# A fused two-layer transformer step: the join of three attention groups by token and in two fp32r parts, and the scan's input sent to DRAM one slot sooner

## The chip, the core and the metric

The kernel runs on one core of one Trainium2 chip. A core has TensorE (matmuls), VectorE, ScalarE and GpSimd, and SyncE, whose queue here issues all DMAs. The metric is the time of one execution on the device in microseconds (us): 1775.94 us for the kernel before, the median of three runs from 1772.67 to 1776.62.

## What is computed

Two layers on one sequence of 1024 tokens of width 1024. The first one has a branch with three groups of four heads of dilated causal attention. Each group gives, for each token and head, a normalised output and the logarithm of its denominator; the groups are then joined by a softmax over these logarithms:

```python
for gi, (window, dilation) in enumerate(B_PATTERNS):      # three groups
    hs = slice(gi * B_HEADS_PER_GROUP, (gi + 1) * B_HEADS_PER_GROUP)
    o_g, lse_g = dilated_window_attention(q[:, :, hs], k[:, :, hs], v[:, :, hs],
                                          rel_bias[:, hs], dilation, window // dilation)
    outs.append(o_g)
    lses.append(lse_g)
o_all = jnp.stack(outs, axis=0)
wts = jax.nn.softmax(jnp.stack(lses, axis=0), axis=0)
y_b = jnp.sum(wts[..., None] * o_all, axis=0).reshape(bn, s, B_OUT_WIDTH).astype(x.dtype)
y_b = y_b * jax.nn.silu(b_z)
```

The second layer has a complex diagonal state space model (the "scan") over an input `u` of 16 groups of 16 channels, next to two kinds of attention. All projections of both layers (`h @ w_in` and the like) are matmuls in float32, and they are most of the work.

## The kernel before

A program is a few *runs* of the class `Dense`, each a row of *slots*. A slot is one half (512 tokens) of one 128-column weight tile: 24 matmuls of 128x128 by 128x512 on L93. Data and weights are each split into a high part rounded to fp32r, the one-instruction float32 format of TensorE ("dense"), and an fp32r remainder; a product is the sum of three partial products over 8 pieces of depth, hence 24. A weight tile comes by DMA (L196) into one buffer `w_raw`; ScalarE rounds its high part (L210) and VectorE takes the remainder (L221). The tile of slots 2n and 2n+1 is prepared this way while earlier ones are multiplied.

All other work hangs on the slots: objects of class `Beside` have a method for each engine that is called at each slot `s`. Each engine's program is the concatenation of these calls in a fixed written order, so the order on an engine never changes at run time; engines meet only at semaphores. On SyncE, `sync(s)` comes before the load of the weight tile that is due at the end of slot `s`. On VectorE a slot has first the `vector_early` calls, then the remainder of the next-but-one weight tile (L221, in the second slot of a tile), then the `vector` calls. On ScalarE a slot has first `scalar_early`, then waits for the slot's matmuls, moves their result (L330) and frees the PSUM bank, rounds a weight tile (L210), and then calls `scalar`. On TensorE the 24 matmuls come first and the `tensor` calls behind them.

The object `Join` sits in the run `Middle`, in its slots 1 and 3 to 8 (`FIRST` = 1, and its own count starts there):

- Slot 1, VectorE (`masks`): the maxima and sums of groups 1 and 2, kept per token in residue order, are spread by masks into operands (L1266, L1272). TensorE: a transpose (L1218) and 12 matmuls (L1222) for the maxima and as many for the sums bring them into 32 rows (8 token tiles x 4 heads) by 128 tokens, for each of the three groups. `places` holds the permutations; `join_sel` is a table of ones that picks a head's row.
- Slot 1, VectorE (`weights`, L1287 to L1297) and ScalarE (one Exp, L1302): the softmax over the groups in the 32x384 layout.
- Slots 3 to 8, one for each of three groups by two pairs of heads, TensorE (L1232): 8 plain float32 matmuls of depth 32 copy a weight to the 64 channels of its head, for 128 tokens each, into banks 2 and 3. VectorE multiplies the group's output by it (L1248), adds up (L1253) and, in the last group, multiplies by the gate (L1256). ScalarE's activation of the first tile that overwrites the groups' outputs waits for the last of it (semaphore `done`).

In the same slots `Modulation` streams 32 parts of `ada_w` (two a slot, L1718), which VectorE multiplies and adds (L1751, L1755).

The object `Ssm` sits in the last run. The first two weight tiles make `u` (slots 0 to 3). SyncE writes `u` to DRAM (L2415) and reads it back in another layout in 8 DMAs (L2420); the matmuls behind slot 7 (L2463) are the first that need it. In that run `self.first` is 7, so the write stands at slot 4 (`i == -3`) and the read at slot 5 (`i == -2`).

Of the kernel before, what the change touches and what calls it, by code (L numbers as in the profile page):

```python
# [16 lines left out]
P = 128  # L17
# [1157 lines left out]
class Join(Beside):  # L1175
# [5 lines left out]
    PLACES = 12 * P + 12  # L1181
    FIRST = 1

    def __init__(self, core, places_dram, sel_dram, maxima, sums, oT, ybT, ident, room):
        self.core, self.places_dram, self.sel_dram, self.ident = core, places_dram, sel_dram, ident
        self.maxima, self.sums, self.oT, self.ybT = maxima, sums, oT, ybT
# [3 lines left out]
        def take(n):  # L1190
            at[0] += n
            return flat[:, at[0] - n:at[0]]

        self.places = take(self.PLACES)
        self.put = self.places[:, 0:12 * P].rearrange("p (n q) -> p n q", q=P)
        self.mask = self.places[:, 12 * P:12 * P + 12]
        self.sel = take(16 * P)[0:32].rearrange("p (t a f) -> p t a f", t=TT, a=2)
        self.spaced = [[take(r * 32).rearrange("p (n t h) -> p n t h", n=r, t=TT) for r in (4, 8)] for _ in range(2)]
        self.m = take(3 * P)[0:32].rearrange("p (g q) -> p g q", g=3)
        self.e = take(3 * P)[0:32].rearrange("p (g q) -> p g q", g=3)  # L1200
        self.top = take(P)[0:32]
        self.loaded, self.masked, self.placed, self.chain, self.topped, self.exped, self.ready, self.spread, \
            self.used, self.done = (core.sem("join_" + n) for n in (
                "loaded", "masked", "placed", "chain", "topped", "exped", "ready", "spread", "used", "done"))

    def turned(self, w):
        return bank(self.core, 6 + w, 1)[0:32, 0:3 * P].rearrange("p (g q) -> p g q", g=3)

    def sync(self, sp, s):
        if s == -1:  # L1210
            sp.dma_start(self.places, self.places_dram).then_inc(self.loaded, 16)
            sp.dma_start(self.sel.rearrange("p t a f -> p (t a f)"), self.sel_dram).then_inc(self.loaded, 16)
# [2476 lines left out]
```

## Time and profile before

| | |
|---|---|
| median of three runs | 1775.94 us (1772.67 to 1776.62) |
| profiled execution: its own time | 1770.18 us |
| its span, first to last instruction | 1768.5 us |
| TensorE busy with matmuls | 1732.2 us, 98% |
| VectorE / ScalarE / GpSimd busy | 52% / 37% / 14% |
| mean granted TensorE clock | 0.997 of 2.4 GHz |
| moved by DMA | 123.10 MB, 70 GB/s on average |

The profile is of one execution. In a timeline each row is a stretch of like instructions: when it starts, how long it lasts, the engine, the line of the kernel, the operation, the tiles as out<-in with their shapes, the count, and, in brackets, how long the engine stood idle before it and what ended that. PE is TensorE's matmul part and PEld its weight loads, which run beside the matmuls. A plain float32 matmul is recorded as two instructions, one with fp32r operands as one. The duration of one matmul is its passage through the array; the distance from one start to the next is what it costs in a stream.

### The profile page before, as it was taken

To read this page: it belongs to the slowest core of one execution; us is meant where nothing else is said; L and a number is where in the kernel's file an instruction comes from. 1 tells how busy PE (TensorE), PEld (TensorE's weight loads), DVE (VectorE), ACT (ScalarE), POOL (GpSimd) and SP (SyncE) were. 2 spreads that over 40 slices of the span, in tenths; PEclk is the share of its full clock that TensorE was granted. 3 is DMA by queue.
4 is the path that set the end of the run, shared out by engine and by line. 5 is a ranking of instruction groups with operands and counts; after the bars stand their busy time and mean duration, and the time that the engine had idled before them with its cause. 6 is when DMAs were issued, how large, how long until landed. Compare 5 with 4: busy or idle time off the path is not lost.

```text
span 1768.5 us, 22516 instructions
## 1 busy us (share of the span) xinstructions
PE 1732.2 (98%) x8828; PEld 1405.8 (79%) x8828; DVE 914.2 (52%) x1525; ACT 652.8 (37%) x1223; POOL 245.4 (14%) x412
## 2 busy tenths in 40 slices
PE   7999999999999999999999999999999999999998
PEld 6788877788888888778888788888787777777786
DVE  5158868564435744763222322467152455657764
ACT  5234438512334432752112211233313463444731
POOL 3012210288701100000000000481000000000000
PEclk9999999999999999999999999999999999999999
DMA  4221110346332200311111221232713111001133
GB/s 144 60 66 48 38 35 2 121 126 190 101 123 62 71 25 13 93 30 48 54 38 55 66 63 30 95 134 85 151 36 99 37 37 37 22 27 48 37 131 107
DMA packets 148277, 123.10 MB, mean 70 GB/s; under 512 B 10556, under 2 KB 133803, under 8 KB 147499
## 3 DMA queue, kind: packets, MB, share of 16 engines
q1 hardware_dynamic: 148170, 121.65, 22.9%
q8 instruction: 71, 1.16, 0.3%
q14 instruction: 36, 0.29, 0.1%
HBM read 108.37 MB, written 13.26 MB: 69 GB/s over the span
## 4 chain that ended last, share of the span: by engine, by line
PE 50%; DVE 4%; DMA 3%; ACT 1%; issue 1%; SPq 0%; DVEq 0%; ACTq 0%
PE psum L93 28%; PE psum L278 7%; PE psum L81 7%; PE psum L2667 2%; PE psum L2698 2%; PE psum L2681 1%; PE psum L1680 1%; DMA w_raw<-w_in 1%; DMA w_raw<-w_out 1%; DMA ssm_U<-u_scratch 0%; PE psum L945 0%; PE psum L931 0%; DVE h2T L2300 0%; PE psum L2463 0%; DVE w_parts L221 0%
## 5 line engine op out<-in xcount | busy, mean ns | idle before, releaser
L93 PE MATMUL psum<-hT,w_parts 128*128 128x512 f32 x3360 | 794.9, 393 | 6.5 <-PEq L61 3.4
L93 PEld LDWEIGHTS psum<-hT,w_parts 128*128 128x128 f32 x3360 | 628.5, 188 | 142.2 <-issue 6.1
L221 DVE TENSOR_TENSOR w_parts<-w_raw,w_parts 128x1024 fp32r<-128x1024 f32 x88 | 111.5, 1267 | 371.9 <-ACT w_parts L210 371.9
L93 PE MATMUL psum<-h2T,w_parts 128*128 128x512 f32 x1248 | 297.1, 394 | 0.0
L93 PEld LDWEIGHTS psum<-h2T,w_parts 128*128 128x128 f32 x1248 | 230.8, 188 | 48.4 <-issue 1.7
L1474 ACT ACTIVATE gate<-psum,cols 128x512 f32<-128x512 f32 x48 | 33.0, 688 | 284.5 <-PE psum L81 284.5
L81 PE MATMUL psum<-y_high,wp_parts 128*128 128x512 f32 x384 | 128.8, 395 | 0.5 <-DVE ya_low L1532 0.3
L210 ACT CAST w_parts<-w_raw 128x1024 fp32r<-128x1024 f32 x88 | 91.6, 1041 | 33.5 <-DMA w_raw<-w_in 28.9
L81 PEld LDWEIGHTS psum<-y_high,wp_parts 128*128 128x128 f32 x384 | 72.0, 188 | 19.2 <-DVE wp_parts L1522 1.7
L278 PE MATMUL psum<-w_parts,y_parts 128*128 128x512 f32 x360 | 82.6, 390 | 0.6 <-DVE w_parts L271 0.6
L403 DVE RECIPROCAL x<-x 128x512 f32<-128x512 f32 x24 | 80.2, 3343 | 0.0
L278 PEld LDWEIGHTS psum<-w_parts,y_parts 128*128 128x128 f32 x360 | 67.3, 188 | 15.1 <-DVE w_parts L271 1.0
L2862 ACT ACTIVATE diff_p<-diff_p,diff_small 128x128 f32<-128x128 f32 (+7 forms) x64 | 49.2, 770 | 81.5 <-DVE diff_small L2792 81.4
L278 PE MATMUL psum<-w_parts,merged_high 128*128 128x512 f32 x240 | 76.0, 392 | 0.0
L1486 DVE TENSOR_TENSOR gate<-psum,gate 128x512 f32<-128x512 f32 x32 | 22.0, 688 | 80.5 <-ACT gate L1474 80.5
L2788 DVE CUSTOM_DVE_ANT_0 diff_p<-psum,far 128x128 f32<-128x128 f32 (+7 forms) x64 | 45.8, 753 | 26.8 <-PE psum L2667 26.7
L1976 POOL MEMSET ssm_cos<- 128x16 f32 x1 | 0.1, 127 | 404.3 <-PE psum L81 404.3
L374 POOL TENSOR_TENSOR sq_parts<-x,sq_parts 128x512 fp32r<-128x512 f32 x24 | 31.0, 1294 | 176.3 <-ACT sq_parts L367 176.3
L278 PEld LDWEIGHTS psum<-w_parts,merged_high 128*128 128x128 f32 x240 | 45.1, 188 | 9.8
L217 DVE TENSOR_TENSOR w_parts<-w_raw,w_parts 128x512 fp32r<-128x512 f32 x32 | 23.7, 772 | 49.8 <-ACT w_parts L206 49.3
L278 PE MATMUL psum<-w_parts,merged_low 128*128 128x512 f32 x112 | 44.1, 393 | 0.2 <-DVE w_parts L271 0.2
L1049 ACT ACTIVATE p<-p,att_small 128x128 f32<-128x128 f32 (+1 forms) x96 | 42.0, 440 | 1.9 <-DVE att_small L987 0.9
(374 smaller groups left out, 2278.4 us busy)
## 6 DMA issues: line engine op xcount, KB each, us to landing
w_raw<-w_in SPq DMA_DIRECT2D x188, 256.0 KB, 3.4
middle_a<-ada_w SPq DMA_DIRECT2D x32, 384.0 KB, 3.6
w_raw<-w_out SPq DMA_DIRECT2D x16, 512.0 KB, 4.1
qkT<-x SPq DMA_DIRECT2D x8, 512.0 KB, 7.7
w_raw<-m_w_kv SPq DMA_DIRECT2D x16, 256.0 KB, 3.1
base<-x SPq DMA_DIRECT2D x8, 512.0 KB, 4.3
x_kept<-x_ring SPq DMA_DIRECT2D x8, 512.0 KB, 2.9
base<-x_kept SPq DMA_DIRECT2D x8, 512.0 KB, 3.6
```

What stands on the lines that cost most here:

```text
L81: last = pe.matmul(out, lhs(a, k), rhs(b, k), start=(k == 0 and n == 0), stop=(k == depth - 1 and n == 2))
L93: last = pe.matmul(out, lhs(a, k), rhs(b, k), start=(n == 0), stop=(n == len(SLOT) - 1))
L210: act.copy(self.parts[:, u, HI, :, :], self.raw[:, :, :]).then_inc(self.high, 2)
L221: dve.tensor_tensor(self.parts[:, u, LO, :, :], self.raw[:, :, :], self.parts[:, u, HI, :, :].bitcast(F32), ALU.subtract).then_inc(self.lo ...
L278: last = pe.matmul(out, lhs(a, k), self.part(b, k)[:, c0:c0 + width], start=(i == 0 and n == 0), stop=(i == KT - 1 and n == 2))
L403: dve.reciprocal(rs, rs).then_inc(run.inverted, 1)
L1049: last = act.activation(into, src, ACT.Exp, bias=self.negative[:, s, h:h + 1], accum_out=sums[:, h:h + 1])
L1474: act.activation(work.gate[:, slot.h, :], run.out(s), ACT.Sigmoid, bias=self.col).then_inc(run.free[slot.bank], 1)
L2667: last = pe.matmul(bank(self.core, 2 * m)[:, c0:c0 + cw], self.qT[rows, h % 2, t * P:(t + 1) * P], self.kT[rows, h % 2, c0:c0 + cw], start ...
L2698: last = pe.matmul(bank(self.core, 6, 1)[:, 0:P], self.pT[:, self.place(b):self.place(b) + P], self.v[:, h % 2, b, :], start=(b == 0), sto ...
L2788: last = dve.tensor_tensor_reduce(self.p[:, s, m, 0:width], bank(self.core, 2 * m)[:, 0:width], self.far[:, D - width:D], 2.0 ** -(5 + h), ...
L2862: last = act.activation(self.p[:, s, m, 0:width], self.p[:, s, m, 0:width], ACT.Exp, bias=self.negative[:, s, m:m + 1], accum_out=self.tot ...
```

## The change

Three parts of `Join` and one number of `Ssm`:

1. **By token.** In slot 1 the permutation is now the stationary operand and the masked values, maxima and sums side by side (64 columns), are the moving one: 12 matmuls (L1238) in place of 2 transposes and 24 matmuls. The results lie by token, 128 partitions by 32 columns for each group, as group 0 already does, so group 0 needs no transpose. The softmax runs on 128 partitions (L1320 to L1330). Behind slot 2 one transpose (L1244) turns the 96 weights of each token into 96 rows (3 groups x 8 token tiles x 4 heads) of 128 tokens.
2. **Masked rows in two dense-mode parts.** At the start of slot 3 VectorE writes these rows eight times side by side, times a 0/1 mask that keeps for each row its own token tile (L1266, 96x1024), ScalarE rounds that to fp32r (L1335), and VectorE takes the remainder directly behind it (L1270). In slots 3 to 8 the spreading is then 4 fp32r matmuls of depth 32 and 512 columns (L1255, L1257: high and low part, for each half of the tokens) in place of 8 plain float32 ones of 128 columns. The table `join_sel` is smaller (96x264 in place of 32x2048) and is rounded to fp32r once (L1342). TensorE waits in slot 3 for the table (`chosen`) and the remainder (`rest`).
3. **The scan's input.** The write of `u` to DRAM stands at slot 3 in place of slot 4. The reads stay at slot 5.

```diff
@@ class Join @@
     def tensor(self, pe, s):
         s -= self.FIRST
         if s == 0:
-            for w, src in enumerate((self.maxima, self.sums)):
-                pe.transpose(self.turned(w)[:, 0, :], src[:, 0:32], self.ident)
-                for g, r in enumerate((4, 8)):
-                    pe.wait_ge(self.masked, 2 * w + g + 1)
-                    for n in range(r):
-                        last = pe.matmul(self.turned(w)[:, g + 1, :],
-                                         self.spaced[w][g][:, n, :, :].rearrange("p t h -> p (t h)"),
-                                         self.put[:, (0, 4)[g] + n, :], start=(n == 0), stop=(n == r - 1))
-                last.then_inc(self.placed, 1)
+            for g, r in enumerate((4, 8)):
+                pe.wait_ge(self.masked, 2 * g + 2)
+                for n in range(r):
+                    last = pe.matmul(bank(self.core, 6, 1)[:, 64 * g:64 * g + 64], self.put[:, (0, 4)[g] + n, :],
+                                     self.spaced[g][:, n, :, :, :].rearrange("p w t h -> p (w t h)"),
+                                     start=(n == 0), stop=(n == r - 1))
+            last.then_inc(self.placed, 1)
+        if s == 1:
+            pe.wait_ge(self.ready, 1)
+            pe.transpose(self.by_head(), self.m.rearrange("p g c -> p (g c)"), self.ident).then_inc(self.turned, 1)
         if 2 <= s < 8:
             g, pair = (s - 2) // 2, s % 2
-            pe.wait_ge(self.ready, 1)
-            if s > 2:
+            rows = slice(32 * g, 32 * g + 32)
+            if s == 2:
+                pe.wait_ge(self.chosen, 1)
+                pe.wait_ge(self.rest, 1)
+            else:
                 pe.wait_ge(self.used, s - 2)
-            for t in range(TT):
-                last = pe.matmul(bank(self.core, 2)[:, t * P:(t + 1) * P], self.sel[:, t, pair, :],
-                                 self.m[:, g, :], start=True, stop=True)
+            for h in range(2):
+                half = slice(h * HALF, (h + 1) * HALF)
+                pe.matmul(bank(self.core, 2 + h, 1), self.sel[rows, pair * P:(pair + 1) * P], self.high[rows, half],
+                          start=True, stop=False)
+                last = pe.matmul(bank(self.core, 2 + h, 1), self.sel[rows, pair * P:(pair + 1) * P],
+                                 self.low[rows, half], start=False, stop=True)
             last.then_inc(self.spread, 1)
 
     def vector_early(self, dve, s):
         if s == self.FIRST:
             self.masks(dve)
+        if s == self.FIRST + 2:
+            dve.wait_ge(self.turned, 1)
+            dve.tensor_tensor(self.wide, self.by_head().unsqueeze(1).to_broadcast([self.ROWS, TT, P]),
+                              self.own.unsqueeze(2).to_broadcast([self.ROWS, TT, P]),
+                              ALU.mult).then_inc(self.widened, 1)
+            dve.wait_ge(self.rounded, 1)
+            dve.tensor_tensor(self.low, self.wide.rearrange("p t q -> p (t q)"), self.high.bitcast(F32),
+                              ALU.subtract).then_inc(self.rest, 1)
...
+    def scalar_early(self, act, s):
+        if s == self.FIRST + 2:
+            act.wait_ge(self.widened, 1)
+            act.copy(self.high, self.wide.rearrange("p t q -> p (t q)")).then_inc(self.rounded, 1)
 
     def scalar(self, act, s):
         if s == self.FIRST:
-            act.wait_ge(self.topped, 1)
+            act.wait_ge(self.topped, 2)
             act.activation(self.m, self.m, ACT.Exp).then_inc(self.exped, 1)
+            act.wait_ge(self.loaded, 32)
+            act.copy(self.sel, self.sel_raw[0:self.ROWS, 0:2 * P]).then_inc(self.chosen, 1)
@@ class Ssm, sync @@
-        if i == -3:
+        if i == -4:
```

What is cut from the diff: the buffers' places, the same two edits inside `masks` (6 instructions now 6, with the same sizes) and `weights` (9 instructions now 10, narrower), and the table in `head_rows`.

On TensorE, from slot 0 of `Middle` to the first spreading, before (`mergedT_49` is the room that `Join` works in, `const` holds the identity):

```order
L93 MATMUL psum<-hT,w_parts 128x512 x48
L1218 MATMUL psum<-const,maxima 32x128
L1222 MATMUL psum<-mergedT_49 32x128 x12
L1218 MATMUL psum<-const,sums 32x128
L1222 MATMUL psum<-mergedT_49 32x128 x12
L93 MATMUL psum<-hT,w_parts 128x512 x48
L1232 MATMUL psum<-mergedT_49 128x128 x8
L93 MATMUL psum<-hT,w_parts 128x512 x24
```

and now:

```order
L93 MATMUL psum<-hT,w_parts 128x512 x48
L1238 MATMUL psum<-mergedT_49 128x64 x12
L93 MATMUL psum<-hT,w_parts 128x512 x24
L1244 MATMUL psum<-const,mergedT_49 96x128
L93 MATMUL psum<-hT,w_parts 128x512 x24
L1255 MATMUL psum<-join_parts_58,join_sel_57 128x512
L1257 MATMUL psum<-join_parts_58,join_sel_57 128x512
L1255 MATMUL psum<-join_parts_58,join_sel_57 128x512
L1257 MATMUL psum<-join_parts_58,join_sel_57 128x512
L93 MATMUL psum<-hT,w_parts 128x512 x24
```

The slot's 24 matmuls are where they were; a transpose stands between slots 2 and 3, and the four spreading matmuls repeat in each of six slots.

On VectorE, from the end of the softmax in slot 1 into slot 3, before (`middle_a` is the sum of `Modulation`, `x_3` the groups' outputs):

```order
L1297 TENSOR_TENSOR mergedT_49<-mergedT_49 32x384
L1751 TENSOR_SCALAR middle_a<-middle_a 128x768 x2
L221 TENSOR_TENSOR w_parts<-w_raw,w_parts 128x1024
L1248 TENSOR_TENSOR x_3<-psum,x_3 128x1024
```

and now:

```order
L1330 TENSOR_TENSOR mergedT_49<-mergedT_49 128x96
L1791 TENSOR_SCALAR middle_a<-middle_a 128x768 x2
L1266 TENSOR_TENSOR mergedT_49<-psum,mergedT_49 96x1024
L1270 TENSOR_TENSOR join_parts_58<-mergedT_49,join_parts_58 96x1024
L221 TENSOR_TENSOR w_parts<-w_raw,w_parts 128x1024
L1281 TENSOR_TENSOR x_3<-psum,x_3 128x1024
```

The two wide instructions stand behind the first pair of `Modulation` and ahead of a weight tile's remainder.

On SyncE, around the write of `u`, as one piece of the difference:

```order
 L196 DMA w_raw<-w_in 128x4x64 x8
+L2455 DMA u_scratch<-ssm_u_7050 128x1024 x2
 L196 DMA w_raw<-w_in 128x4x128 x2
-L2415 DMA u_scratch<-ssm_u_7082 128x1024 x2
-L2420 DMA ssm_U_7100<-u_scratch 16x16x128 x8
+L2460 DMA ssm_U_7068<-u_scratch 16x16x128 x8
 L196 DMA w_raw<-w_in 128x4x128 x10
```

The write now stands ahead of a weight tile's two loads; the reads stay behind them.

## Rows read from the trace of the kernel before

**Rows 1.** The page: busy time, and shares of the chain that ended last.

```profile
PE 1732.2 (98%) x8828; PEld 1405.8 (79%) x8828; DVE 914.2 (52%) x1525; ACT 652.8 (37%) x1223; POOL 245.4 (14%) x412
PE 50%; DVE 4%; DMA 3%; ACT 1%; issue 1%; SPq 0%; DVEq 0%; ACTq 0%
```

**Rows 2.** Timeline of TensorE's matmuls, slot 1 to slot 9 of the run.

```profile
335.72 0.27 PE L1218 MATMUL psum<-const,maxima 128*32 128x128 f32 x1
335.92 2.81 PE L1222 MATMUL psum<-mergedT 128*32 128x128 f32 x24
...
341.61 11.17 PE L93 MATMUL psum<-hT,w_parts 128*128 128x512 f32 x48
352.71 2.05 PE L1232 MATMUL psum<-mergedT 32*128 32x128 f32 x16
354.69 5.73 PE L93 MATMUL psum<-hT,w_parts 128*128 128x512 f32 x24
360.35 2.05 PE L1232 MATMUL psum<-mergedT 32*128 32x128 f32 x16
...
390.91 2.05 PE L1232 MATMUL psum<-mergedT 32*128 32x128 f32 x16
392.89 5.73 PE L93 MATMUL psum<-hT,w_parts 128*128 128x512 f32 x24
398.85 21.34 PE L93 MATMUL psum<-hT,w_parts 128*128 128x512 f32 x93 [0.23 <-ACT x L330]
```

**Rows 3.** Groups of weight loads and matmuls: busy us, mean ns of one.

```profile
L93 PEld LDWEIGHTS psum<-hT,w_parts 128*128 128x128 f32 x3360 | 628.5, 188 | 142.2 <-issue 6.1
...
L1736 PE MATMUL psum<-const,middle_a 128*128 128x1 f32 x32 | 3.6, 248 | 0.0
L2484 PE MATMUL psum<-ssm_ys,glu_w 128*128 128x512 f32 x16 | 7.0, 592 | 0.0
```

**Rows 4.** Timeline of VectorE in slots 1, 2, 7 and 8.

```profile
335.30 0.36 DVE L1266 TENSOR_TENSOR mergedT<-maxima,mergedT 128x64 f32<-128x64 f32 x2 [3.05 <-DMA mergedT<-join_sel]
...
338.06 1.23 DVE L221 TENSOR_TENSOR w_parts<-w_raw,w_parts 128x1024 fp32r<-128x1024 f32 x1 [1.46 <-ACT w_parts L210]
...
344.45 1.13 DVE L1751 TENSOR_SCALAR middle_a<-middle_a 128x768 f32<-128x768 f32 x2
...
385.01 1.23 DVE L221 TENSOR_TENSOR w_parts<-w_raw,w_parts 128x1024 fp32r<-128x1024 f32 x1 [2.96 <-ACT w_parts L210]
...
389.81 1.94 DVE L1755 SCALAR_TENSOR_TENSOR middle_a<-middle_a 128x768 f32<-128x768 f32 x2
393.00 1.22 DVE L1248 TENSOR_TENSOR x<-psum,x 128x1024 f32<-128x1024 f32 x1 [1.25 <-PE psum L1232]
```

**Rows 5.** Timeline of ScalarE at the end of the join.

```profile
396.81 1.28 ACT L330 ACT_TABLE_LOAD   x1 [11.90 <-DVE x L1256]
398.11 1.15 ACT L330 ACTIVATE x<-psum 128x512 f32<-128x512 f32 x2
```

**Rows 6.** DMA issues from 334 to 345 us: KB each, median us to landing.

```profile
middle_a<-ada_w SPq DMA_DIRECT2D x2, 384.0 KB, 7.3
```

**Rows 7.** Timeline around the scan's input: the DMA queue, ScalarE and TensorE.

```profile
1242.36 19.48 SPq L196 DMA_DIRECT2D w_raw<-w_in  x10
...
1255.91 1.07 ACT L330 ACTIVATE ssm_u<-psum 128x512 f32<-128x512 f32 x1
...
1261.93 0.92 SPq L2415 DMA_DIRECT2D u_scratch<-ssm_u  x2
...
1266.40 1.04 ACT L210 CAST w_parts<-w_raw 128x1024 fp32r<-128x1024 f32 x1
1267.32 3.76 SPq L2420 DMA_DIRECT2D ssm_U<-u_scratch  x8
...
1278.43 2.05 PE L2463 MATMUL psum<-ssm_U,ssm_Gt 128*128 128x128 f32 x16 [1.68 <-DMA ssm_U<-u_scratch]
```

**Rows 8.** DMA issues from 1240 to 1280 us.

```profile
ssm_U<-u_scratch SPq DMA_DIRECT2D x8, 128.0 KB, 5.6
```

More of the change, by code:

```diff
@@ L1192, in take, with take_round @@
             return flat[:, at[0] - n:at[0]]
+        def take_round(name, shape):
+            at[0] += math.prod(shape[1:])
+            return core.over(name, shape, room_at + 4 * (at[0] - math.prod(shape[1:])), F32R)
         self.places = take(self.PLACES)
@@ L1196, in __init__, with by_token, by_head @@
         self.mask = self.places[:, 12 * P:12 * P + 12]
[L1197 to L1207, printed above, removed]
+        self.sel_raw = take(2 * P + TT)
+        self.own = self.sel_raw[0:self.ROWS, 2 * P:2 * P + TT]
+        self.spaced = [take(r * 64).rearrange("p (n w t h) -> p n w t h", n=r, w=2, t=TT) for r in (4, 8)]
+        self.m = take(self.ROWS).rearrange("p (g c) -> p g c", g=3)
+        self.e = take(self.ROWS).rearrange("p (g c) -> p g c", g=3)
+        self.top = take(32)
+        self.wide = take(S)[0:self.ROWS].rearrange("p (t q) -> p t q", t=TT)
+        at[0] = -(-at[0] // 8) * 8
+        self.sel = take_round("join_sel", [P, 2 * P])[0:self.ROWS]
+        parts = take_round("join_parts", [P, 2, S])
+        self.high, self.low = parts[0:self.ROWS, HI, :], parts[0:self.ROWS, LO, :]
+        assert at[0] <= 6 * S
+        self.loaded, self.masked, self.placed, self.chain, self.topped, self.exped, self.ready, self.turned, \
+            self.widened, self.chosen, self.rounded, self.rest, self.spread, self.used, self.done = (
+                core.sem("join_" + n) for n in (
+                    "loaded", "masked", "placed", "chain", "topped", "exped", "ready", "turned", "widened", "chosen",
+                    "rounded", "rest", "spread", "used", "done"))
+    def by_token(self):
+        return bank(self.core, 6, 1)[:, 0:128].rearrange("p (g w c) -> p w g c", g=2, w=2)
+    def by_head(self):
+        return bank(self.core, 7, 1)[0:self.ROWS, 0:P]
     def sync(self, sp, s):
@@ L3198, in first_block @@
         stat = core.sb(stack, "mem_stat", [P, 4])
-        middle = Middle(core, A, const, cols, x1, mergedT, hT, later, stack)
+        middle = Middle(core, A, const, cols, x1, mergedT, merged_at, hT, later, stack)
         w_middle = SplitTiles(core, stack, [(len(middle.tiles), lambda j: middle.tiles[0].view)], shares=w,
@@ L3359, in prepare @@
         by_rows = lambda name: A[name].rearrange("(k p) n -> p k n", p=P)
[L3360 removed]
+        self.join = Join(core, A["places"], A["join_sel"], maxima, sums, oT, ybT, self.ident, mergedT[:, 0:6, :],
+                         self.merged_at)
         modulation = Modulation(core, room_a, A["c"], by_rows("ada_w"), self.col("ada_b"), A["ada_gate_b"],
@@ L3600, in head_rows @@
 def head_rows():
-    sel = np.zeros((32, TT, 2, P), np.float32)
+    rows = np.zeros((3, TT, 4, 2 * P + TT), np.float32)
+    for n, h in enumerate(HEAD_AT):
+        rows[:, :, n, P * (h // 2) + 64 * (h % 2):P * (h // 2) + 64 * (h % 2) + 64] = 1.0
     for t in range(TT):
-        for n, h in enumerate(HEAD_AT):
-            sel[4 * t + n, t, h // 2, 64 * (h % 2):64 * (h % 2) + 64] = 1.0
-    return sel.reshape(32, 2 * TT * P)
+        rows[:, t, :, 2 * P + t] = 1.0
+    return rows.reshape(12 * TT, 2 * P + TT)
 def distances(rows, width, at, limit):
```

53 lines of the change are left out of this document (28 added, 25 removed).

## The prediction

> **What bounds the kernel now.** I read the page first: its busy line gives TensorE 98% of the span, VectorE 52% and ScalarE 37%, and the chain that ended last runs over TensorE more than over all others together [rows 1]. So time comes from two places only: instructions taken out of TensorE's stream, and its few waits. I then read TensorE's timeline through the slots in which the join sits [rows 2]. The reader is to see there that it has no idle bracket up to 398.85 us: the join's matmuls there are paid in full. Last I read the timeline around the scan's input, where TensorE does wait: 1.68 us ahead of the first scan matmul, for the reads of `u` [rows 7].
>
> Two figures carry everything. Forty-eight slot matmuls run from 341.61 to 352.71 us, 11.10 us, and twenty-four from 354.69 to 360.35, 5.66 us; the difference is 5.44 us for 24, 0.227 us each, and 0.22 us are left over at the change to the join's matmuls [rows 2]. The join's 16 instructions take from 352.71 to 354.69, 1.98 us, so a slot's spreading costs 0.22 + 1.98 = 2.20 us, and the period is 7.64 us (352.71 to 360.35) [rows 2]. Within it the spacing is (2.05 - 0.27)/15 = 0.119 us (a single matmul lasts 0.27, as the first row shows), 1.90 us for 16, so 0.08 us are left at the change back: 0.30 us of a slot's 2.20 are changes.
>
> **The spreading, slots 3 to 8.** Now there are 4 fp32r matmuls of 512 columns. At the spacing of the slot matmuls they take 4 x 0.227 = 0.91 us; with the same 0.30 us of changes, a slot pays 1.21 and saves 0.99. Six slots save 5.9 us. No row has an fp32r matmul of depth 32. The favourable bound is no change cost at all (0.91, saving 1.29 a slot, 7.7 in all). The other bound is the plain float32 matmul of 512 columns: 16 recorded instructions, 8 matmuls, busy 7.0 us, 0.875 us each [rows 3], which would make a slot 3.80 us, 1.60 more than now. I take 0.227, because nearest in type and columns are the 48 of rows 2.
>
> **The permutation, slot 1.** It occupied 335.72 to 341.61, 5.89 us [rows 2]. The 24 old instructions of a set are (2.81 - 0.27)/23 = 0.110 us apart. The new ones move 64 columns in place of 128, but load 128 columns of weights. The nearest row is L1736: 32 instructions with 128x128 weights and a single moving column, busy 3.6 us, 0.113 us each [rows 3]. So the weights set that pace and fewer columns don't help: 24 x 0.113 = 2.7 us, with 0.2 for the change 2.9, saving 3.0. Bounds: 2.7 us without the change, and 3.5 with a wait. The wait is possible because group 1 now needs both masked values: the masks began at 335.30 when the table landed and a pair takes 0.36 us [rows 4], so two pairs end at 336.0, 0.3 after 335.72. A smaller table (101 KB in place of 256) should land sooner, which hides it.
>
> The Trainium skill, "TensorEngine Tiling (Array Packing)", section "Instruction Overhead", says that a matmul has about 60 cycles of overhead and that one column takes as long as 60. By that alone, as an estimate, 24 instructions of 64 columns would cost about 24 x 0.03 = 0.7 us and the saving would be 5.2. L1736 contradicts it for float32 with full weights, so the sum goes by the row.
>
> **The softmax and the transpose.** The old chain on VectorE was over by 344.45 us, when the next instruction began without a wait [rows 4]; it began behind the weight remainder that starts at 338.06 and lasts 1.23. TensorE is at the end of slot 2 at 335.72 + 2.9 + 5.44 = 344.1. The new chain has 10 instructions in place of 9 but on 32 to 96 columns in place of 128 to 384, so it ends well before; even at the old length it would cost 0.4 us. The transpose itself costs the 0.20 us from 335.72 to 335.92 [rows 2] and a change of 0.22: 0.45 us (0.2 to 0.6).
>
> **The two parts, start of slot 3.** This adds three wide instructions in a row that TensorE waits for at the end of slot 3. Durations of the same size: 1.22 us for VectorE out of PSUM (L1248) [rows 4], 1.04 for ScalarE's rounding (L210) [rows 7], 1.23 for the remainder (L221) [rows 4]. With the transpose's own 0.3 and 0.15 for hand-overs they end 3.9 us after the slot's start, and the slot lasts 5.44: hidden, with 1.5 us to spare. Ahead of them on VectorE stands the pair L1751, which needs `ada_w`: landed 7.3 us after its issue [rows 6], and in any case before 344.45 [rows 4]. Done by then it ends at 345.6 at the latest, which would still leave the chain finished at 349.2, ahead of 344.5 + 5.44 = 349.9. Behind them stands the remainder of a weight tile that waits for the end of slot 3 anyway. If the cover is gone, each us of lateness costs one us, once. The table's rounding on ScalarE (96x256) lies in slot 1 in front of a result that comes 5 us later: nothing.
>
> **What is late next.** Shorter slots leave VectorE less time. In slot 7 its work runs without a gap from the remainder at 385.01 to 389.81 + 1.94 = 391.75, that is from 1.74 to 8.48 us behind the start of the spreading, which is one period (7.64) before 390.91; in slot 8 it then waited 1.25 us for the spreading [rows 4]. With a period of 5.44 + 1.21 = 6.65 the spreading of slot 8 is finished at 6.65 + 1.07 = 7.72 us (three spacings and a last matmul of 0.39), and VectorE comes only at 8.48: about 0.7 us late. ScalarE's first activation onto the groups' outputs waits for exactly this multiplication chain, loads a table, and TensorE's slot 10 waits for it, already before: slot 9 begins at 392.89, so slot 10 could begin at 398.33 and begins at 398.85 [rows 2, 5]. So the lateness is paid: 0.7 us lost. In the slots before it VectorE has no third multiplication and there is room.
>
> **The scan's input.** The write was issued at 1261.93, behind a weight tile's loads, which waited for a buffer; the reads, which wait for its landing, went out 5.4 us later at 1267.32, landed 5.6 us after issue in the middle, and the last at 1278.4 [rows 7, 8]. `u` itself was ready at 1255.91 + 1.07 = 1256.98. Now the write goes out then and lands 5.4 us later, at 1262.4, and the reads, still behind the tile's loads (issued until 1242.36 + 19.48 = 1261.84), go out at about 1262.4, 4.9 us sooner. TensorE wants them at 1278.43 - 1.68 = 1276.75, so even with 3 us lost to the tile's loads beside them the 1.7 us go. The new wait on SyncE stands ahead of these loads, but they wait for a later event already. That tile is rounded at 1266.40 with no wait before it [rows 7].
>
> **The sum.** -3.0 (permutation) + 0.45 (transpose) - 5.9 (spreading) + 0.7 (VectorE in slot 8) - 1.7 (scan) = -9.5 us. The profiled execution, 1770.18 us with a span of 1768.5, would become 1760.7. It lay 5.8 below the median of the runs; from the median 1775.94 I forecast 1766.4. Its own range, with spreading and slot 8 together between 4.3 and 6.7 saved and the scan between 1.3 and 1.9, is -11.5 to -7.5, and with some 2 us of scatter of a median 1763 to 1770.
>
> **Rivals.**
> - *The scan's wait stays.* The reads now meet the weight tile's loads in the same DMA engines. For it: they took 11 us from first issue to last landing even alone. Against it: 4.9 us are won and only 1.7 needed. It leaves -7.8: 1768.1.
> - *Weights not loaded beside matmuls.* If the weight loads of depth 32 stood between the matmuls, each of the 24 would pay the duration of a load more, 0.19 us by the slot matmuls' own [rows 3]. A slot then costs 4 x 0.417 + 0.30 = 1.97 and saves 0.23, VectorE is in time again, and the sum is -3.0 + 0.45 - 1.4 - 1.7 = -5.7: 1770.3. Against it: the slot matmuls, all on the same rows, keep 0.227 with a load for each. The Trainium skill, "TensorE: Matmul & The Clock Gate", section "The mechanism" of Part 3, says that a weight load overlaps a running matmul only when its row group differs; the spreading keeps to one group a slot, so by that rule this rival would hold. The trace speaks against the rule.
> - *Slower: no dense pace at depth 32.* If an fp32r matmul on 32 rows ran in the passes of plain float32, 0.875 us [rows 3], the six slots would cost 6 x 1.60 = 9.6 more in place of 5.9 less: -3.0 + 0.45 + 9.6 - 1.7 = +5.3, 1781.3. It decides from 0.63 us a matmul on (9.5/24 = 0.40 above 0.227; the lateness in slot 8 then also goes, so a little above that). For it: every fp32r row of this trace has depth 128. Against it: the fp32r rows are single instructions and plain ones two, which is a matter of type, not of depth.
>
> **How the numbers follow.** Forecast 0.68, scan's wait stays 0.12, weights not beside 0.11, no dense pace 0.04; 0.05 for something unseen. A change below 0.2% (3.6 us) can't be told from none in a measurement of this kernel. The forecast and the first rival are beyond it almost surely (0.77 of 0.80), the second rival mostly (0.07 of 0.11): faster 0.84, the same 0.11, slower 0.05. The range from 1762 to 1771 holds the forecast's own and reaches over the first two rivals; the slower case is left out.
>
> **What the new profile would show.** The spreading rows L1255 and L1257: four instructions a slot, 0.227 apart, a period of 6.65 us in slots 4 to 7. L1238: 24 instructions in 2.9 us or less. No idle on TensorE at L1255 released by L1270. VectorE's L1281 in slot 8 without idle ahead of it, and TensorE's wait ahead of slot 10 grown by some 0.7 us. No wait at the first scan matmul. The forecast is wrong if the period stays above 7.4 us, if the wide chain ends behind slot 3, or if the downstream slots do not begin about 7.8 us sooner from 399 us on.

## The result, and the profile after

| | median us | lowest to highest | runs |
|---|---|---|---|
| before | 1774.67 | 1772.67 to 1776.62 | 4 |
| after | 1765.22 | 1764.13 to 1767.30 | 4 |

The ratio of after to before is 0.9945, with a 95% interval from 0.9932 to 0.9958: 9.4 us, or 0.55%, faster. The forecast was 1766.4 us and 9.5 us faster. The profiled execution of after took 1767.3 us, with a span of 1765.6; that of before had 1770.18 and 1768.5. So the two profiles are only 2.9 us apart where the medians are 9.4 apart. Part of the work below is to find the rest.

The page after, busy time and chain [rows 1]:

```profile
PE 1727.1 (98%) x8731; PEld 1398.5 (79%) x8731; DVE 915.1 (52%) x1528; ACT 653.4 (37%) x1225; POOL 247.0 (14%) x412
PE 53%; DVE 3%; ACT 1%; issue 1%; DMA 1%; SPq 0%; DVEq 0%; ACTq 0%
```

TensorE has 97 instructions fewer (6 times 12 in the spreading, 24 in the permutation, one transpose) and is still the bound. Its timeline through the join, which answers to [rows 2] (start us, busy us, engine, line, operation, count, and in brackets the idle time before):

```profile
325.30 11.22 PE L93 MATMUL psum<-hT,w_parts 128*128 128x512 f32 x48
336.36 2.79 PE L1238 MATMUL psum<-mergedT 128*128 128x64 f32 x24
338.95 5.74 PE L93 MATMUL psum<-hT,w_parts 128*128 128x512 f32 x24
344.52 0.27 PE L1244 MATMUL psum<-const,mergedT 128*96 128x128 f32 x1
344.55 5.70 PE L93 MATMUL psum<-hT,w_parts 128*128 128x512 f32 x24
350.18 0.50 PE L1255 MATMUL psum<-join_parts,join_sel 32*128 32x512 f32 x1
350.52 0.40 PE L1257 MATMUL psum<-join_parts,join_sel 32*128 32x512 f32 x1
350.76 0.39 PE L1255 MATMUL psum<-join_parts,join_sel 32*128 32x512 f32 x1
351.00 0.39 PE L1257 MATMUL psum<-join_parts,join_sel 32*128 32x512 f32 x1
351.32 5.73 PE L93 MATMUL psum<-hT,w_parts 128*128 128x512 f32 x24
...
384.95 0.39 PE L1257 MATMUL psum<-join_parts,join_sel 32*128 32x512 f32 x1
385.27 5.74 PE L93 MATMUL psum<-hT,w_parts 128*128 128x512 f32 x24
391.67 28.60 PE L93 MATMUL psum<-hT,w_parts 128*128 128x512 f32 x125 [0.66 <-ACT x L330]
```

The reader is to see three things. The permutation is over in 2.59 us (336.36 to 338.95). The four matmuls of a slot start 0.34, 0.24 and 0.24 us apart, and the next slot's spreading starts at 356.98 us, so the period is 6.80. No matmul of the join has an idle bracket. From the start of slot 1 to that of slot 10 it is 391.67 - 325.30 = 66.37 us, where before took 398.85 - 324.67 = 74.18; its slot 1 starts with this row:

```profile
324.67 11.21 PE L93 MATMUL psum<-hT,w_parts 128*128 128x512 f32 x48
```

The two parts on VectorE and ScalarE, the chain that the forecast placed in slot 3, are below; the view is the timeline of those two engines.

```profile
344.83 1.22 DVE L1266 TENSOR_TENSOR mergedT<-psum,mergedT 96x1024 f32<-96x1024 f32 x1 [0.33 <-PE psum L1244]
...
347.17 1.22 DVE L1270 TENSOR_TENSOR join_parts<-mergedT,join_parts 96x1024 fp32r<-96x1024 f32 x1 [1.11 <-ACT join_parts L1335]
...
385.78 1.22 DVE L1281 TENSOR_TENSOR x<-psum,x 128x1024 f32<-128x1024 f32 x1
...
389.63 1.28 ACT L330 ACT_TABLE_LOAD   x1 [10.64 <-DVE x L1289]
```

The remainder is finished at 348.4, 1.8 us before TensorE wants it. L1281 in slot 8 has lost the 1.25 us of idle that it had in [rows 4]: VectorE is now late there, and TensorE's idle ahead of slot 10 has grown from 0.23 to 0.66 us.

Around the scan's input [rows 7] (the DMA queue, ScalarE, TensorE):

```profile
1235.17 18.32 SPq L196 DMA_DIRECT2D w_raw<-w_in  x8
...
1249.08 1.04 ACT L210 CAST w_parts<-w_raw 128x1024 fp32r<-128x1024 f32 x1 [9.53 <-DMA w_raw<-w_in]
1252.18 23.63 PE L93 MATMUL psum<-h2T,w_parts 128*128 128x512 f32 x96 [2.89 <-ACT ssm_u L330]
1253.59 1.33 SPq L2455 DMA_DIRECT2D u_scratch<-ssm_u  x2
1261.28 3.94 SPq L2460 DMA_DIRECT2D ssm_U<-u_scratch  x8
...
1275.65 1.95 PE L2503 MATMUL psum<-ssm_U,ssm_Gt 128*128 128x128 f32 x16
```

The wait at the first scan matmul is gone. But a wait of 2.89 us, which before did not have, stands in front of it: the third weight tile of the run is issued at 1235.17 and its rounding begins only 13.9 us later, at 1249.08. (Below, the time from a tile's issue to the start of its rounding is called its landing time.)

### The profile page after: what moved, and what is told of

It is laid out like the page before. It is cut to its first block, busy times and chain, and to the rows that moved or that the text cites. A ratio compares the mean times of both kernels' runs of the same rounds, so it can differ in the third digit from the quotient of the medians.

```text
span 1765.6 us, 22322 instructions
## 1 busy us (share of the span) xinstructions
PE 1727.1 (98%) x8731; PEld 1398.5 (79%) x8731; DVE 915.1 (52%) x1528; ACT 653.4 (37%) x1225; POOL 247.0 (14%) x412
## 4 chain that ended last, share of the span: by engine, by line
PE 53%; DVE 3%; ACT 1%; issue 1%; DMA 1%; SPq 0%; DVEq 0%; ACTq 0%
PE psum L93 29%; PE psum L278 8%; PE psum L81 7%; PE psum L2707 2%; PE psum L2738 2%; PE psum L2721 1%; PE psum L1720 1%; DMA w_raw<-w_in 1%; PE psum L945 0%; PE psum L931 0%; DVE h2T L2340 0%; PE psum L2503 0%; PE psum L2524 0%; PE psum L920 0%; SPq L196 0%
```

## The experiments

The kernels of one group ran on the same chip and shared the runs of before.

**First group**: before 1774.98 us median (17 runs).

`e0_after_again`, the changed kernel unaltered.

> The changed kernel once more, unaltered. Its profile had two losses that the prediction had not: TensorE stood 2.9 us before the fifth slot of the last run, because the third weight tile landed late, and the granted clock fell to about 0.57 for 4 us behind the one-column matmuls near 450 us. Theory A (the late tile belongs to the order of the DMAs, which is the same in every execution): the wait of 2 to 4 us and the lower clock near it appear again. Theory B (it was a chance of that one execution): no such wait, and the end comes 4 to 5 us sooner than in the profile seen, at a span near 1761. Ratio to the kernel before 0.993 to 0.996 by both.

Measured: 1764.01 us (1762.85 to 1766.67), ratio 0.9936 [0.9922, 0.9950]. Slot 1 to slot 10 took 66.33 us. The wait at `ssm_u` was there again, but with 1.28 us, the tile landing after 12.1 us; the lower clock near 450 us and behind the wait was not. So the late tile is no chance of one execution, and its size varies.

`e1_join_only`:

```
-        if i == -4:
+        if i == -3:
```

> The join alone is changed; the write of u stands at slot 4 as before. Forecast theory (join worth 7.8 us, scan 1.7 us): 7.8 us faster than before, and the wait of about 1.7 us before the first scan matmul is back. Rival (the scan's write is worth nothing because its gain is lost in the same DMA crowd): the same time as the full change, 9.5 us faster than before.

Measured: 1768.06 us (1764.67 to 1769.97), ratio 0.9956 [0.9943, 0.9970]: 6.9 us faster than before by the medians. The scan's wait is back and the one at `ssm_u` is not there:

```profile
1232.93 38.44 PE L93 MATMUL psum<-h2T,w_parts 128*128 128x512 f32 x168
1272.95 2.05 PE L2503 MATMUL psum<-ssm_U,ssm_Gt 128*128 128x128 f32 x16 [1.59 <-DMA ssm_U<-u_scratch]
```

`e2_scan_only`, the kernel before with the write a slot sooner:

```
-        if i == -3:
+        if i == -4:
```

> The kernel before with only the write of u at slot 3. Forecast theory: the wait before the first scan matmul goes, 1.7 us faster (ratio 0.999), which is at the edge of what can be told. Rival: the reads meet the weight tile's loads and land no sooner, time unchanged and the wait stays.

Measured: 1773.62 us (1767.49 to 1776.70), ratio 0.9984 [0.9972, 0.9996]: 1.4 us by the medians. The scan's wait is gone, and 1.67 us at `ssm_u` have come.

```profile
1261.78 22.03 PE L93 MATMUL psum<-h2T,w_parts 128*128 128x512 f32 x96 [1.67 <-ACT ssm_u L330]
1283.64 1.95 PE L2463 MATMUL psum<-ssm_U,ssm_Gt 128*128 128x128 f32 x16
```

`e3_m_later`, the changed kernel, with `glu`, `M` and `M_swap` (2.25 MB by the DMA issues) loaded a slot later, so behind the weight tile that came late:

```
     def sync(self, sp, s):
         N, i = SSM_GROUPS, s - self.first
-        if s == -1:
+        if s == 0:
             sp.dma_start(self.glu, self.glu_dram)...
```

> The changed kernel with the four large loads for the scan (glu weights, M and its two swapped halves, 2.25 MB) issued at slot 0 of the last run, behind the load of the third weight tile and no longer ahead of it. Theory A (the third tile is late because it queues behind these loads): the tile lands about 4 us after issue, the 2.9 us wait of TensorE and the lower clock behind it go, and the kernel is 2 to 5 us faster than the full change. Rival: the loads only move the crowd onto the next tile or the scan's own write, and another wait of 2 us or more appears there; time unchanged.

Measured: 1764.01 us (1762.82 to 1764.64), ratio 0.9933 [0.9920, 0.9946]. The tile is issued at 1235.61 and rounded from 1240.51, 4.9 us later. Both waits are gone:

```profile
1232.97 38.44 PE L93 MATMUL psum<-h2T,w_parts 128*128 128x512 f32 x168
...
1240.51 1.05 ACT L210 CAST w_parts<-w_raw 128x1024 fp32r<-128x1024 f32 x1 [0.61 <-DMA w_raw<-w_in]
...
1271.25 1.95 PE L2503 MATMUL psum<-ssm_U,ssm_Gt 128*128 128x128 f32 x16
```

From the matmuls of `ssm_col` (L2452 before, L2492 after) to the first scan matmul, before needed 43.44 us, the full change 46.30 and 43.11 in its two profiles, and this kernel 41.55. `e6_mixed` and `e10_last_first` below have the loads in the same later place: their tile lands after 4.8 and 4.6 us, and the stretch takes 41.55 and 41.54. So with the three loads behind it the tile is in time in all three profiles, and with them ahead it took 8.8 us or more in all ten. The 2 to 5 us that were expected do not show in the time: the medians can't tell 1764.01 from the 1764.01 and 1765.22 of the full change.

**Second group**: before 1774.15 us median (18 runs).

`e4_plain_spread`, no rounded parts in the spreading:

```
-                pe.matmul(bank(self.core, 2 + h, 1), self.sel[rows, ...], self.high[rows, half],
-                          start=True, stop=False)
-                last = pe.matmul(bank(self.core, 2 + h, 1), self.sel[rows, ...],
-                                 self.low[rows, half], start=False, stop=True)
+                last = pe.matmul(bank(self.core, 2 + h, 1), self.sel_raw[rows, ...],
+                                 self.whole[rows, half], start=True, stop=True)
```

> The changed kernel, but the spreading uses the whole (unsplit) wide rows in plain float32: two matmuls of 512 columns a slot in place of four fp32r ones. The rounding and the remainder are still computed, and not read. Theory: a plain float32 matmul of 512 columns costs 0.875 us (16 recorded instructions of L1776 and its like, 7.0 us) whatever its depth. A slot's spreading then occupies 2 x 0.875 + 0.30 = 2.05 us and the period in slots 4 to 7 is 7.5 us, where the changed kernel has 6.80. That is 0.7 us on each of six slots, 4.2 us, less the 0.44 us of VectorE's lateness in slot 8, which goes: about 3.8 us slower than the changed kernel, 1768. Rival: the time depends on depth, and a plain matmul on 32 rows costs as little as an fp32r one (0.24 us a pass and half): the period stays at 6.8 or below and so does the time. Second rival: depth 32 is a penalty in plain float32, and a slot costs more than 2.2 us.

Measured: 1769.44 us (1767.04 to 1771.66), ratio 0.9972 [0.9960, 0.9983].

```profile
350.39 1.98 PE L1256 MATMUL psum<-mergedT 32*128 32x512 f32 x4
352.30 5.74 PE L93 MATMUL psum<-hT,w_parts 128*128 128x512 f32 x24
357.97 1.98 PE L1256 MATMUL psum<-mergedT 32*128 32x512 f32 x4
...
390.20 5.74 PE L93 MATMUL psum<-hT,w_parts 128*128 128x512 f32 x24
396.19 24.05 PE L93 MATMUL psum<-hT,w_parts 128*128 128x512 f32 x105 [0.26 <-ACT x L330]
```

The period is 7.58 us (forecast 7.5), against 7.64 of before and 6.80 of the full change. So wide rows alone, with 4 recorded instructions a slot in place of 16, would have been worth almost nothing: 0.06 us a slot. The gain comes from the fp32r parts. Depth 32 gives no discount in plain float32: the four recorded instructions take 1.91 us (350.39 to 352.30), where 0.437 us each, the price at depth 128 [rows 3], would be 1.75. Slot 9 to slot 10 is 5.99 us, and slot 1 to slot 10 takes 396.19 - 325.55 = 70.64 us, 4.3 more than in the full change (3.8 were expected).

`e5_twice`:

```
-            for h in range(2):
+            for h in (0, 1, 0, 1):
```

> The changed kernel, but the four fp32r matmuls of each slot's spreading are issued twice, the second pass writing the same values again. Theory: an fp32r matmul on 32 rows with its own weight load costs 0.227 to 0.24 us in a row of them, as one on 128 rows does, and the rest of the 1.36 us that a slot's spreading occupies is paid once. So four more cost 0.91 to 0.96 us a slot: period 7.7 to 7.8 us, 5.5 to 5.8 us in all, less 0.44 us since VectorE is then in time in slot 8 (the distance from slot 9's start to slot 10's returns from 6.40 to 5.96 us): 5.0 to 5.3 slower than the changed kernel, 1769. Rival: weight loads on the same rows stand between the matmuls, 0.42 us each: 10 us slower. Rival on slot 8: the 6.40 us are not VectorE's lateness, and stay.

Measured: 1768.38 us (1765.49 to 1773.35), ratio 0.9968 [0.9958, 0.9978].

```profile
349.41 0.50 PE L1255 MATMUL psum<-join_parts,join_sel 32*128 32x512 f32 x1
...
351.15 0.39 PE L1257 MATMUL psum<-join_parts,join_sel 32*128 32x512 f32 x1
351.47 5.71 PE L93 MATMUL psum<-hT,w_parts 128*128 128x512 f32 x24
357.11 0.50 PE L1255 MATMUL psum<-join_parts,join_sel 32*128 32x512 f32 x1
...
389.95 5.73 PE L93 MATMUL psum<-hT,w_parts 128*128 128x512 f32 x24
395.92 24.29 PE L93 MATMUL psum<-hT,w_parts 128*128 128x512 f32 x106 [0.24 <-ACT x L330]
```

The period is 7.70 us. Four more matmuls cost 0.90 us, 0.225 each: the price that the forecast took from the 128-row matmuls holds at 32 rows, each with its own weight load. Slot 9 to slot 10 is back at 5.97 us. Slot 1 to slot 10 is 395.92 - 324.57 = 71.35 us, 5.0 above the full change's 66.37, as expected. The medians say 4.4 against `e0_after_again`, which is of another group.

`e6_mixed`, on top of `e3_m_later`:

```
                 last = pe.matmul(bank(self.core, 4, 1)[:, j:j + 1], ...)
+                if j in (4, 10):
+                    h = (4, 10).index(j)
+                    pe.matmul(bank(self.core, 5 + h, 1), self.ones, ...)
```

> The changed kernel with the loads of glu, M and M_swap a slot later (as in e3_m_later), and in the modulation's sum the two matmuls of 512 columns (L1779) stand among the sixteen of one column, behind the fifth and the eleventh, and not behind all. Theory: the clock granted to TensorE falls to its lower level around 450 us in most profiles because some 3.6 us of one-column matmuls stand in one piece ahead of it; broken up by wide ones, the granted clock stays at 1.00 from 440 to 470 us, and the time is 1 to 2 us below that of the changed kernel with the later loads, 1762 to 1763. Rival: the fall at 450 us comes whatever the order, or moves to another place: same time, 1764, and rows below 1.00 between 440 and 470 us.

Measured: 1763.74 us (1762.72 to 1765.37), ratio 0.9940 [0.9926, 0.9953]. The theory fell. The stretch has a clock at the lower of its two levels (0.50 of 2.4 GHz is 1.2 GHz) all the same. The view is that of windows: the stretch, its length, busy us and instructions of PE, PEld, DVE, ACT and POOL, then the granted clock, the DMA share and GB/s:

```profile
452.00:456.00 4.00, 4.00 (x15) 3.29 (x14) 0.98 (x3) 1.61 (x3) 3.53 (x7) 0.50 0.45 131
456.00:460.00 4.00, 4.00 (x15) 3.17 (x14) 1.32 (x3) 0.00 (x0) 3.69 (x5) 0.72 0.33 135
```

`e7_wider_places`, 128 moving columns in 20 of the permutation's 24 recorded instructions:

```
-                    last = pe.matmul(bank(self.core, 6, 1)[:, 64 * g:64 * g + 64], self.put[...],
-                                     self.spaced[g][:, n, :, :, :]...
+                    c = 2 if n < r - 1 else 1
+                    last = pe.matmul(bank(self.core, 6, 1)[:, 64 * g:64 * g + 64 * c], self.put[...],
+                                     self.spaced[g][:, n:n + c, :, :, :]...
```

> The changed kernel, but in the permutation of slot 1 the matmuls move 128 columns in place of 64 (the next rank's values beside their own, into columns that nobody reads), but for the last of each group: 20 of 24 recorded instructions. Theory: the load of 128 columns of weights sets the pace, not the moving columns, so L1238 still takes 2.6 us from its start to that of the next slot's matmuls (0.11 us an instruction). Rival: columns count at the rate of the plain 512-column matmul (0.437 us an instruction, 0.055 us for 64 columns): 20 x 0.055 = 1.1 us more, 3.7 us. The time of the kernel can't tell them apart, the profile can.

Measured: one run, 1768.84 us.

```profile
339.03 2.79 PE L1239 MATMUL psum<-mergedT 128*128 128x128 f32 x24
341.63 5.74 PE L93 MATMUL psum<-hT,w_parts 128*128 128x512 f32 x24
```

2.60 us, as with 64 columns (2.59). From 64 to 128, the moving columns cost nothing here.

**Third group**: before 1775.21 us median (9 runs).

`e8_join_only_again`, the same edit as `e1_join_only`.

> The same kernel as e1_join_only (the new join, the scan's write where it was), profiled once more. In all six profiles with the write one slot sooner and the three loads (glu, M, M_swap) in their old place, TensorE stands for 1.3 to 2.9 us at `ssm_u`, since the third weight tile lands 11.7 to 13.9 us behind its issue; in the two with the write in its old place it landed after 9.1 and 9.2 us and nothing stood. Theory: this goes with the write's place, so here the tile lands after about 9 us, there is no wait released by `ssm_u`, and the wait of some 1.6 us at the first scan matmul is back. Rival: the two without it were chance: a tile landing after 11 us or more and a wait at `ssm_u` appear here as well.

Measured: one run, 1768.78 us. The rival holds. The tile, issued at 1236.96, is rounded from 1248.19, 11.2 us later, and a wait appears at `ssm_u`, though a small one; the scan's wait is there too:

```profile
1248.19 1.05 ACT L210 CAST w_parts<-w_raw 128x1024 fp32r<-128x1024 f32 x1 [7.01 <-DMA w_raw<-w_in]
...
1251.34 22.05 PE L93 MATMUL psum<-h2T,w_parts 128*128 128x512 f32 x96 [0.41 <-ACT ssm_u L330]
1275.37 3.07 PE L2503 MATMUL psum<-ssm_U,ssm_Gt 128*128 128x128 f32 x16 [1.99 <-DMA ssm_U<-u_scratch]
```

`e9_before_again`, the kernel before.

> The kernel before, profiled once more. Its first profile was of its fastest execution but one (1770.2 against a median of 1774) and lost only 4.5 us to stretches below a granted clock of 1.00, where the changed kernel's lost 8.6 and 8.0. Theory: the difference between the profiles of before and after (2.9 us at the end, against 9.4 in the medians) is that: a profile of before near its median shows 7 us or more lost at the lower clock, and a span some 8 to 10 us above 1764.9. Rival: before really loses less at the lower clock, and this profile shows 4 to 5 us again. On the tile: it lands about 9 us behind its issue, no wait at `ssm_u`, 1.7 us at the scan.

Measured: 1776.28 us, span 1774.5. Its mean granted clock was 0.994, the first profile's 0.997. The view of spans and clocks (core, span, mean granted clock):

```profile
core 0: 1774.5 us, clock 0.994
```

1 - 0.997 of 1768.5 us is 5.3 us, 1 - 0.994 of 1774.5 is 10.6, and with the 0.995 of after's 1765.6 it is 8.8. The first profile of before was one of an execution that lost less: its 1770.18 us are below each of the 44 times of before in the three groups (the lowest is 1770.58). This one has a tile landing after 8.8 us, no wait at `ssm_u`, and 2.20 us at the first scan matmul.

`e10_last_first`, on top of `e3_m_later`: VectorE issues the join's multiplications of slot 8 directly behind those of slot 7, ahead of the modulation's pair.

```
-        if 2 <= s < 8:
+        for s in ((), (s,), (6, 7))[(2 <= s < 7) + (s == 6)]:
```

> The changed kernel with the three loads a slot later (as e3_m_later), and on VectorE the join's three multiplications of slot 8 stand directly behind those of slot 7, ahead of that slot's modulation pair. Theory: VectorE then comes to the spreading of slot 8 as soon as it is finished, 0.5 us sooner than now, ScalarE's table load and first activation follow as much sooner, and the distance from slot 9's start to slot 10's on TensorE falls from 6.40 to about 5.97 us, as in the kernels with a longer spreading (5.97 and 5.99). 0.4 us less, too little for the medians: 1763.6. Rival: the 0.96 us between slot 9's end and slot 10 in the changed kernel has another cause, and 6.40 stays.

Measured: 1763.09 us (1761.81 to 1766.41), ratio 0.9938 [0.9924, 0.9952].

```profile
385.02 5.74 PE L93 MATMUL psum<-hT,w_parts 128*128 128x512 f32 x24
390.99 9.35 PE L93 MATMUL psum<-hT,w_parts 128*128 128x512 f32 x40 [0.23 <-ACT x L330]
```

Slot 9 to slot 10 is 5.97 us. It has the lowest median of all, but its interval overlaps that of the full change: not shown to be faster.

## Why the prediction was right, step by step

The forecast's time and the join's steps held. Four sizes within the join were off by 0.3 to 0.9 us each and offset one another, and the scan's part freed its wait without making its stretch shorter by as much. So the mechanism of the join was right, and that the sums came out at 7.8 us, and near 9.5 in all, is in part luck.

| term | forecast | measured | from |
|---|---|---|---|
| permutation | -3.0 | -3.3 | 5.89 [rows 2] to 2.59 us |
| transpose | +0.45 | +0.1 | 338.95 to 350.18 is 11.23 us, two slots 11.10 |
| spreading | -5.9 | -5.0 | 6 x (7.64 - 6.80) |
| VectorE in slot 8 | +0.7 | +0.4 | slot 9 to 10: 6.40 against 5.96 us |
| to slot 10 | -7.8 | -7.8 | 66.37 against 74.18 us |
| scan's wait | -1.7 | the wait of 1.6 to 2.2 is gone, 1.3 to 2.9 are given back at `ssm_u` | see below |

*The permutation.* L1736 was the right row: 24 instructions in 2.59 us are 0.108 us each, and `e7_wider_places` has the same with twice the columns. The change of 0.2 us was not paid on top. That the weights set this pace, as the prediction reads it, is not shown: the old L1222, with weights of only 32 columns, has its instructions 0.110 us apart too [rows 2]. What the rows show is about 0.11 us for each recorded plain float32 instruction, with 1, 64 or 128 moving columns and with 32 or 128 columns of weights. The estimate of 0.7 us after the Trainium skill ("TensorEngine Tiling (Array Packing)", "Instruction Overhead") did not come true; for these plain float32 instructions the measurement decides against it.

*The transpose.* It was mis-sized: a single transpose in the stream costs 0.1 us, not 0.20 and a change of 0.22. In before the 0.20 us of L1218 were the distance to the next instruction; the change, taken from the spreading, did not show.

*The spreading.* The price of a matmul was right (0.225 by `e5_twice`, 0.227 forecast). What was mis-sized is the change. A slot pays 6.80 - 5.44 = 1.36 us, and 4 x 0.225 = 0.90 leaves 0.46 us where I took 0.30 from a slot with another kind of instruction. The rows show where it lies: 0.22 us ahead of the four, as forecast, and 0.32 from the last of the four to the next slot, as forecast too (0.227 + 0.08), but the first distance is 0.34 us, 0.1 more than the other two. Six slots of 0.16 us are the 0.9 us that were missing. The timeline of weight loads differs at the same place: the loads of the second to fourth matmul start 0.23 us ahead of their matmuls (350.29 for 350.52), the first one, behind the matmuls of 128 rows, only together with its own (350.18), the load part having stood 0.35 us. That this is what the 0.1 us pay for was not tested.

*VectorE in slot 8.* The mechanism was right and is shown from both sides: a longer spreading (`e4_plain_spread`, `e5_twice`) and an earlier multiplication (`e10_last_first`) each bring the distance back to 5.97 to 5.99 us. The size was 0.4 in place of 0.7. VectorE comes at 385.78, 8.43 us behind the start of slot 7's spreading (a period of 6.80 before 384.15), as forecast (8.48); but the spreading of slot 8 is finished only at 384.95 + 0.39 = 385.34, 7.99 us behind it, not at 7.72.

*The wide chain in slot 3.* It was hidden with 1.8 us to spare; 1.5 were forecast. `ada_w` came late (VectorE's pair waited 1.33 us for it) and the cover held.

*The scan's input.* The step "the write goes out when `u` is ready, and the wait goes" held: no profile with the sooner write has the wait. What failed is that this makes the stretch 1.7 us shorter: the forecast assumed that nothing upstream is late, and the third weight tile is. With the sooner write and the three loads ahead of the tile there are six profiles (`after`, `e0_after_again`, `e2_scan_only`, `e4_plain_spread`, `e5_twice`, `e7_wider_places`): the tile lands after 11.7 to 13.9 us, and TensorE stands at `ssm_u` for 2.89, 1.28, 1.67, 1.44, 1.70 and 2.40 us. From the first `ssm_col` matmul to the first scan matmul they take 46.30, 43.11, 43.48, 43.24, 43.53 and 44.19 us. The four with the write in its old place take 43.44 and 43.91 (before) and 43.29 and 44.39 (the join alone). The medians of the two sets, 43.5 and 43.7, are 0.2 us apart: in this stretch the sooner write is worth next to nothing as long as the loads stand ahead of the tile. With the loads behind it, the same write comes with 41.5 us in three profiles, some 2 us less than before.

Whether the late tile belongs to the write's place is not settled. Before it took 9.1 and 8.8 us, with the new join alone 9.2 and 11.2, with the sooner write and the loads ahead of it 11.7 or more in every profile. `e8_join_only_again` shows that 11 us happen without the write. The write is issued behind the tile's landing, so it can't crowd it out directly. What is shown is the remedy: with the three loads behind the tile it lands in 4.6 to 4.9 us.

*Where the profiles' 2.9 us come from.* Between the first profiles of before and after, the parts are +0.6 us ahead of slot 1 (324.67 and 325.30), -7.8 from slot 1 to slot 10, +1.5 from the modulation's sum to the `ssm_col` matmuls, +2.9 from there to the first scan matmul, and -0.1 behind it. The second profile of before and that of `e0_after_again` have spans of 1774.5 and 1764.9, 9.6 apart. By their milestones: -7.9 us between slot 1 and slot 10 (74.24 to 66.33), -2.2 from the modulation's sum to the `ssm_col` matmuls (785.1 to 782.9), -0.8 to the first scan matmul, and +1.4 ahead of slot 1, where nothing is changed (slot 1 begins at 326.69 and 328.11). The same stretch from the sum to `ssm_col` took 781.6 us in the first profile of before and 783.2 in that of after, with the same instructions in all four. That scatter of 3.5 us, no part of the change, goes with the granted clock. Taking, for each 4 us row of the view of windows, 4 us times 1 minus the granted clock as its loss, the stretch loses 1.7 (first of before), 5.2 (second), 3.4 (after) and 3.4 us (`e0_after_again`); without these it takes 779.9, 779.9, 779.7 and 779.5. In after such rows look like this, the second of them right behind the wait of 2.89 us, where it costs another 1.6 us or so (the 96 matmuls there take 23.63 us and 22.04 in `e0_after_again`):

```profile
452.00:456.00 4.00, 4.00 (x15) 2.88 (x14) 2.75 (x5) 0.00 (x0) 3.61 (x6) 0.79 0.23 77
...
1252.00:1256.00 4.00, 3.82 (x10) 3.04 (x11) 0.00 (x0) 2.48 (x4) 0.00 (x0) 0.57 0.81 224
```

So of the 9.4 us of the medians 7.8 are the join, which each pair of profiles shows, and a remainder of 1.6 is left. By the medians of the first group the join alone accounts for 6.9 us (1774.98 - 1768.06) and the sooner write alone for 1.4, together 8.3, while the full change has 11.0 there (1774.98 - 1764.01). The remainder is no larger than the scatter of the clock and of the late tile. The profiles do not put it down to the sooner write, whose stretch is not shorter by that much, and no more is claimed for it.

*The rivals.* "The scan's wait stays" is out as to the wait; what it would have cost, the 1.7 us, the stretch did not win all the same. "Weights not loaded beside matmuls" is out: it asked for 0.42 us a matmul, and it is 0.24, with loads of 0.18 us each, all on one row group within a slot. By the rule of the Trainium skill that the prediction names ("TensorE: Matmul & The Clock Gate", Part 3, "The mechanism") they should not have overlapped; the same section also lets a load into the background weight buffer be pulled ahead, which this trace does not contradict. These are the loads of the spreading (the groups of weight loads):

```profile
L1257 PEld LDWEIGHTS psum<-join_parts,join_sel 32*128 32x128 f32 x12 | 2.2, 184 | 0.3
L1255 PEld LDWEIGHTS psum<-join_parts,join_sel 32*128 32x128 f32 x12 | 2.2, 182 | 2.4 <-issue 2.1
```

"No dense pace at depth 32" is out for fp32r; plain float32 pays its own price at depth 32 as at 128, as `e4_plain_spread` shows.

## What to carry to other kernels

Price a matmul by the measured row nearest to it in type and width, not by its share of the array: 32 rows cost what 128 do, and up to 128 moving columns a recorded plain float32 instruction cost about 0.11 us whatever its columns. Wide float32 matmuls in place of many narrow ones gave 0.06 us a slot; the two fp32r parts in place of those gave another 0.78. When a DMA is moved or a stage shortened, look for the transfer that TensorE waits for next, and put large loads that nobody needs yet behind it.

A profile is of one execution. Before reading a difference of a few us off two of them, compare their mean granted clock, and the distance between two fixed places that the change does not touch.

## What the runs showed that was not expected

- A single transpose (L1244) cost about 0.1 us in the stream of fp32r matmuls, while a change to the four fp32r matmuls of 32 rows and back cost 0.46 us, more than the 0.30 us of a change to 16 plain float32 ones.
- The granted clock falls for a few us at like places: around 20 and 710 us in all thirteen profiles, near 450 in eleven, near 268 in five. Ahead of 20, 710 and 268 TensorE had stood idle (2.8, 3.4 and 1.8 us in `e9_before_again`; after stood 1.8 us there too and had no fall); at 450 it had not, there one-column matmuls came before. Breaking those up by wide ones did not keep the fall away (0.50 in `e6_mixed`). What does is open.
- One weight tile of 0.5 MB landed after 4.6 to 4.9 us or after 8.8 to 13.9, depending on whether `glu`, `M` and `M_swap` were issued behind or before it, and, with these before it, for a reason that stays open.
